# Decode attention with a running maximum, value products three steps behind the keys, and page rings of five

## Chip, core and metric

The kernel runs on one core of one Trainium2 chip. The metric is the device time of one execution in microseconds (us), the median over several executions of the same program. A core has four engines for computing that run beside each other, each with its own queue of instructions: TensorE (PE in the profile, its weight loads PEld), VectorE (DVE), ScalarE (ACT) and GpSimd (POOL). SyncE (SP) only issues transfers. Engines wait for each other through semaphores.

## What is computed

One layer of a hybrid decoder is computed for 1024 prompt tokens and for 8 sample sequences of 8 new tokens each. Only the sample attention over the paged cache is touched by the change:

```python
def diff_attend_sample(q, k, v, lam, k_past, v_past):     # 8 sequences, 8 tokens, 4 heads x 2 sub-heads
    s_past = jnp.einsum('bqhcd,bkhcd->bhcqk', q, k_past).astype(F32) * scale      # 4096 past keys
    s_new = jnp.where(jnp.tril(...), jnp.einsum('bqhcd,bkhcd->bhcqk', q, k) * scale, -jnp.inf)
    a = jax.nn.softmax(jnp.concatenate([s_past, s_new], axis=-1), axis=-1)
    w = a[:, :, 0] - lam * a[:, :, 1]
    return einsum(w[..., :P], v_past) + einsum(w[..., P:], v)
```

Each sequence has 32 pages of 128 keys and values in a pool in HBM, found through a page table. A page is 256 KB of keys and 256 KB of values. All data are 32-bit floats.

## The kernel before, in words

The program runs an input projection, the gated linear attention (to about 432 us), then `attention` (432 to 869 us), and then the dense stages (output projection, feed-forward, embedding) from 869 us to the end. Between `attention` and the dense stages stands the end of a block, which every engine has to reach.

`attention` does the prompt attention and the sample attention interleaved, in an order written out by hand: each engine has a loop over steps `t`, with `STEPS = NKV + LAG + 1`. A group is four pages of one sequence (512 keys); there are `NG = 8` groups to a sequence and `NKV = 64` groups in all. `LAG = NG + 1 = 9`, so there are 74 steps.

What belongs to the keys of group `t`, in step `t`: TensorE turns the four pages for each of four heads (`turn_keys`, line 1587, 16 transposes) into a ring of three PSUM banks; ScalarE copies heads 0 to 2 (`take_keys`, line 1470) and VectorE head 3 (line 1751) to `dec_kt`. One step later TensorE forms the scores of all heads and tokens in bank 6, `S_BANK` (`score`, line 1599). In step `t+2` VectorE takes the row maximum of that bank (line 1756) and copies it to `dec_s` (`copy_scores`, line 1762); the copy frees the bank for the next `score`. When the eight groups of a sequence and its new keys (`score_new`, `take_new`, lines 1609 and 1772) are there, VectorE forms the maximum of the whole sequence.

What belongs to the values of group `v = t - LAG`, in step `t`: ScalarE takes the exponentials from `dec_s` with that maximum as bias (`exps`, line 1481); TensorE turns them (`turn_p`, line 1622, and once per sequence `turn_new_p`, line 1616); VectorE copies them (line 1790); TensorE multiplies them with the value pages (`values`, line 1641), accumulating over all eight groups of a sequence in bank 7, `O_BANK`. At the end of a sequence VectorE scales the result (`finalize`, line 1807), TensorE merges the sub-heads (`merge`, line 1649) and ScalarE stores it (`copy_os`, line 1492).

The prompt attention has 32 units (head, block of queries), two steps for each: `prompt_scores` (line 1547), mask and maxima on VectorE (lines 1711 to 1715), `prompt_exps` (line 1446), and for the unit before `prompt_turn` (line 1560), `copy_weights` (line 1456), for the one before that `prompt_out` (line 1569). Its last piece is in step 66. The norm of its output (`norm_prompt`, line 1735) is done on VectorE in steps 68 to 71, after a logarithm and an exponential on ScalarE in step 67 (lines 1521, 1524).

The order within step `t` on TensorE: keys of heads 0 and 1, `prompt_out` (even steps) or `prompt_turn` (odd steps), keys of heads 2 and 3, `merge`, `turn_new_p`, `turn_p`, rest of `prompt_turn`, `prompt_scores`, `score`, `score_new`, `values`.

Page rings: keys and values have four slots each (`KR`, `VR`). SP loads keys (line 1302 and the next) in the order of the groups: groups 0 to 2 come before the attention starts, group 3 at its start, then the queries of two prompt units, the prompt's values `att_v` (2 MB) and the new values `dec_new_v`, and group `n` from 4 on once the keys of group `n - 4` are turned. GpSimd issues the value pages; groups 0 to 3 wait for the keys of group `2n`, later ones for the values of group `n - 4`. After the last keys SP loads two tiles of `w_out`.

The semaphore waits that matter here, quoted:

```python
1597:    pe.wait_ge(d["s_taken"], k)                              # score: S_BANK copied
1592:    pe.wait_ge(d["ring_act"], ring.emptied["keys", k, 2])    # score: keys copied
1420:    gp.wait_ge(d["ring_filled"], ring.filled(("keys", 2 * n, H - 1)))
1422:    gp.wait_ge(d["pv_done"], n - VR + 1)
```

Of the kernel before, what the change touches and what calls it, by code (L numbers as in the profile page):

```python
# [1193 lines left out]
def attention_memory(m):  # L1194
# [13 lines left out]
    m.kr, o = m.at("dec_k", o, [P, KR, 4, H * P])  # L1208
    m.vr, o = m.at("dec_v", o, [P, VR, 4, H * P])
# [4 lines left out]
    m.osc, o = m.at("dec_osc", o, [P, DV])  # L1214
# [4 lines left out]
    m.ss, o = m.at("dec_s", o, [P, PAST + NS])  # L1219
    m.kt, o = m.at("dec_kt", o, [P, 2, H, 4 * PAGE])  # L1220
    m.os, o = m.at("dec_os", o, [32, DB, DV])
# [12 lines left out]
KR, VR, QR, PRE = 4, 4, 4, 3  # L1234
NG = NPG // 4
NKV = DB * NG
LAG = NG + 1
# [18 lines left out]
class Ring:  # L1256
# [4 lines left out]
    def __init__(self):  # L1261
# [9 lines left out]
        for t in range(STEPS):  # L1271
# [11 lines left out]
            b, last = divmod(t - NG, NG)  # L1283
            if last == 0 and 0 <= b < DB:
                use(("new_s", b), "dve")
# [13 lines left out]
def load_pages(eng, ids, cache, ring, slot, sem, n):  # L1299

    for p in range(4):
        page = eng.value_load(ids[0:1, 4 * n + p:4 * n + p + 1], min_val=0, max_val=POOL - 1)
        eng.dma_start(ring[:, slot, p:p + 1, :], cache[bass.ds(page, 1)].rearrange("o t f -> t o f")).then_inc(sem, 16)  # L1303
# [15 lines left out]
def attention(nc, io, m, ps, scr, sems):  # L1319
# [12 lines left out]
    names = ("states_stored new_v_in zero_done qb_ready ring_filled ring_act ring_dve s_full s_taken mx negm exp_done "  # L1332
             "expn_done pv_done final scale_set")
# [23 lines left out]
    mx, esum, ssum, cs, negm = (m.sc[:, 24:33], m.sc[:, 34:52].rearrange("p (u g) -> p u g", u=2), m.sc[:, 52:54],  # L1357
                                m.sc[:, 54:56], m.sc[:, 56:58])
# [18 lines left out]
    with nc.Block() as block:  # L1377

        @block.sync
        def _(sp):  # L1380
# [21 lines left out]
            sp.wait_ge(s["o_done"], NU)  # L1402
# [10 lines left out]
        def _(gp):  # L1413
# [18 lines left out]
        def _(act):  # L1432
# [39 lines left out]
            def exps(v):  # L1472
                b, g = divmod(v, NG)
                if g == 0:
                    act.wait_ge(d["negm"], b + 1)
                    if b >= 2:
                        act.wait_ge(d["final"], 4 * (b - 2) + 1)
                act.wait_ge(d["s_taken"], v + 1)
                if v >= 2:
                    act.wait_ge(d["ring_filled"], ring.filled(("p", v - 2)))  # L1480
                act.activation(m.pg[:, v % 2, :], m.ss[:, 512 * g:512 * g + 512], ACT.Exp, scale=SC,
                               bias=negm[:, b % 2:b % 2 + 1], accum_out=esum[:, b % 2, g:g + 1]).then_inc(d["exp_done"], 1)
                if g == 0:
                    if b:
                        act.wait_ge(d["ring_filled"], ring.filled(("new_p", b - 1)))
                    act.activation(m.pn[:, 0:NS], m.ss[:, PAST:PAST + NS], ACT.Exp, scale=SC,
                                   bias=negm[:, b % 2:b % 2 + 1], accum_out=esum[:, b % 2, NG:NG + 1]
                                   ).then_inc(d["expn_done"], 1)
# [5 lines left out]
            for t in range(STEPS):  # L1494
                v = t - LAG
                n, c = divmod(t, 2)
                first_group = 0 <= v < NKV and v % NG == 0
                if 0 <= v < NKV and not first_group:
                    exps(v)
# [5 lines left out]
                prompt_exps(t - 1)  # L1505
                if first_group:
                    exps(v)
# [20 lines left out]
        def _(pe):  # L1528
# [49 lines left out]
            def turn_keys(t, h):  # L1578
# [7 lines left out]
                for p in range(4):  # L1586
                    ins = pe.transpose(ring_bank(key)[:, p * P:p * P + P], m.kr[:, t % KR, p, h * P:h * P + P], ident)  # L1587
                ins.then_inc(d["ring_filled"], 1)

            def score(k):  # L1590
# [5 lines left out]
                if k:  # L1596
                    pe.wait_ge(d["s_taken"], k)
# [27 lines left out]
            def values(v):  # L1625
                b, g = divmod(v, NG)
                if g == 0:
# [3 lines left out]
                    else:  # L1631
                        pe.wait_ge(d["final"], 4 * b)
                    for h in range(H):
                        pe.matmul(O_BANK[32 * h:32 * h + 32, 0:DV], m.ptn[:, 32 * h:32 * h + 32],
                                  m.vs[:, h * DV:h * DV + DV], start=True, stop=False, tile_position=(0, 32 * h),
                                  skip_group_check=True)
                pe.wait_ge(d["ring_dve"], ring.emptied["p", v])
# [1509 lines left out]
```

## Time and profile before

| what | value |
|---|---|
| three executions | 1883.73 us median (1881.60 to 1884.62) |
| span of the profiled execution | 1880.3 us |
| TensorE busy over the span | 1773.0 us (94%) |
| VectorE, ScalarE, GpSimd busy | 63%, 39%, 18% |
| attention stage (first key transpose to first instruction of the dense stages) | 433.8 to 869.3 us |
| moved by DMA between 500 and 800 us | 105.63 MB, 352 GB/s |

The end-to-end time of the profiled execution itself isn't listed; its span is 1880.3 us, and the three timed executions lie 1.3 to 4.3 us above that. In the rows, a time ahead of a group is the start in us from the span's start, "idle before" is how long the engine had nothing, with what ended that idle time. Matmuls are pipelined and overlap: the start of one to the start of the next tells more than their own durations.

### The profile page before, as it was taken

Reading aid. Unit: us, or ns where it says so; the run is one execution under the profiler, and the core shown is the slowest. Engines: PE = TensorE matmul, PEld = TensorE weight load, DVE = VectorE, ACT = ScalarE, POOL = GpSimd, SP = SyncE. Lnnn points to the kernel's source line nnn. Section 1 sums busy time; section 2 is a strip of 40 time slices with the busy share of each in tenths; the row PEclk is TensorE's granted clock in tenths of the full one; section 3 lists DMA queues with packets and bytes.
Section 4 is the critical chain, followed back from the end, with each engine's and each line's share of the span. In section 5 each row is a group of like instructions: output and inputs, shape, how many; then the busy total and the mean of one; then the engine's idle time right before and its main releaser. Section 6 shows DMA issues by size and latency. Waiting matters only on the chain.

```text
span 1880.3 us, 35481 instructions
## 1 busy us (share of the span) xinstructions
PE 1773.0 (94%) x13062; PEld 1639.1 (87%) x13062; DVE 1192.5 (63%) x1946; ACT 735.6 (39%) x1418; POOL 341.2 (18%) x360
## 2 busy tenths in 40 slices
PE   6999999996999999996999999999999999999998
PEld 6999999984666667665998999999999999999997
DVE  4223742475777777765458876667677878699443
ACT  5113322564655565653225333222323424245320
POOL 1111331001233333332111211211121000000110
PEclk9999999898999999998999999999999999999998
DMA  5323551227999999977111222222222424232121
GB/s 162 108 80 82 141 140 56 61 83 236 330 350 354 346 357 360 353 231 226 35 45 46 80 69 81 81 70 69 81 70 69 157 81 134 74 106 86 47 69 48
DMA packets 232923, 265.73 MB, mean 141 GB/s; under 512 B 16162, under 2 KB 173428, under 8 KB 232756
## 3 DMA queue, kind: packets, MB, share of 16 engines
q1 hardware_dynamic: 211988, 195.36, 33.2%
q0 software_dynamic: 20768, 68.17, 10.7%
q8 instruction: 101, 1.65, 0.4%
q14 instruction: 66, 0.54, 0.1%
HBM read 229.79 MB, written 29.21 MB: 138 GB/s over the span
## 4 chain that ended last, share of the span: by engine, by line
PE 45%; DVE 6%; ACT 1%; issue 1%; DMA 1%; POOL 0%; DVEq 0%; ACTq 0%
PE psum L2518 33%; PE psum L150 10%; DVE x_second_lo L2532 1%; DVE unit_lo L1910 1%; DMA x_first_hi_raw<-scratch_z 1%; PE psum L2197 0%; PE psum L2894 0%; DVE x_second_lo_raw L2536 0%; DVE rstd_and_products L2576 0%; DVE x_first_lo L2532 0%; DVE h L2576 0%; ACT unit_hi L1904 0%; DVE rstd_and_products L2009 0%; DVE x_lo L2226 0%; DMA w_raw<-in_w_ple_gate 0%
## 5 line engine op out<-in xcount | busy, mean ns | idle before, releaser
L2518 PE MATMUL psum<-x_second_hi,unit_hi 128*128 128x364 f32 x924 | 304.5, 330 | 8.0 <-DVE x_second_lo L2532 4.6
L2518 PE MATMUL psum<-x_second_hi,unit_lo 128*128 128x364 f32 x924 | 303.4, 328 | 0.0
L2518 PE MATMUL psum<-x_second_lo,unit_hi 128*128 128x364 f32 x924 | 303.4, 328 | 0.0
L1303 POOL DMA_DIRECT2D dec_v<-in_cache_v x256 | 137.6, 538 | 288.1 <-issue 282.2
L150 PE MATMUL psum<-x_hi,w_hi 128*128 128x364 f32 x768 | 182.0, 345 | 5.8 <-DVE x_lo L2226 5.8
L2518 PEld LDWEIGHTS psum<-x_second_hi,unit_hi 128*128 128x128 f32 x924 | 173.8, 188 | 10.8 <-issue 5.7
L2518 PE MATMUL psum<-x_first_hi,unit_hi 128*128 128x364 f32 x528 | 173.7, 329 | 0.6 <-DVE x_first_lo L2532 0.6
L2518 PEld LDWEIGHTS psum<-x_second_hi,unit_lo 128*128 128x128 f32 x924 | 174.0, 188 | 0.0
L2518 PEld LDWEIGHTS psum<-x_second_lo,unit_hi 128*128 128x128 f32 x924 | 173.7, 188 | 0.0
L2518 PE MATMUL psum<-x_first_hi,unit_lo 128*128 128x364 f32 x528 | 173.5, 329 | 0.0
L2518 PE MATMUL psum<-x_first_lo,unit_hi 128*128 128x364 f32 x528 | 173.2, 328 | 0.0
L150 PE MATMUL psum<-x_hi,w_lo 128*128 128x364 f32 x768 | 170.2, 330 | 0.0
L150 PE MATMUL psum<-x_lo,w_hi 128*128 128x364 f32 x768 | 169.8, 329 | 0.0
L1470 ACT ACTIVATE dec_kt<-psum 128x512 f32<-128x512 f32 x192 | 108.6, 599 | 154.6 <-PE psum L1587 154.6
L1904 ACT ACTIVATE unit_hi<-unit_sums 128x512 fp32r<-128x512 f32 (+1 forms) x136 | 83.3, 618 | 217.2 <-PE psum L2518 184.7
L1587 PE MATMUL psum<-consts,dec_k 128*128 128x128 f32 x1024 | 139.3, 281 | 20.2 <-DMA dec_k<-in_cache_k 8.8
L2397 POOL TENSOR_TENSOR w_raw<-w_raw,gains 128x1024 f32<-128x1024 f32 x42 | 88.7, 2111 | 379.6 <-DMA w_raw<-in_w_ffn_gate 210.8
L1904 ACT ACTIVATE unit_hi<-w_raw 128x512 fp32r<-128x512 f32 (+1 forms) x136 | 82.5, 617 | 178.2 <-PE psum L2518 155.8
L1587 PEld LDWEIGHTS psum<-consts,dec_k 128*128 128x128 f32 x1024 | 115.2, 143 | 39.2 <-issue 15.7
L150 PEld LDWEIGHTS psum<-x_hi,w_hi 128*128 128x128 f32 x768 | 131.5, 189 | 15.2 <-DVE x_lo L2226 6.2
L150 PEld LDWEIGHTS psum<-x_lo,w_hi 128*128 128x128 f32 x768 | 133.9, 189 | 0.0
L150 PEld LDWEIGHTS psum<-x_hi,w_lo 128*128 128x128 f32 x768 | 133.8, 189 | 0.0
(313 smaller groups left out, 3313.3 us busy)
## 6 DMA issues: line engine op xcount, KB each, us to landing
dec_k<-in_cache_k SPq DMA_DIRECT2D x256, 256.0 KB, 5.7
dec_v<-in_cache_v POOLq DMA_DIRECT2D x256, 256.0 KB, 5.5
w_raw<-in_w_in SPq DMA_DIRECT2D x25, 512.0 KB, 3.9
scratch_z<-ffn_hidden SPq DMA_DIRECT2D x22, 546.0 KB, 2.8
w_raw<-in_w_ffn_gate SPq DMA_DIRECT2D x22, 512.0 KB, 3.8
w_raw<-in_w_ffn_up SPq DMA_DIRECT2D x22, 512.0 KB, 3.8
w_raw<-in_w_ffn_down SPq DMA_DIRECT2D x16, 512.0 KB, 4.0
feat_swap<-feat_n SPq DMA_DIRECT2D x32, 136.5 KB, 2.4
```

The costliest lines, as they stand in the source:

```text
L150: ins = pe.matmul(out[:, c, 0:SPAN], w(k), x(k)[:, c * SPAN:c * SPAN + SPAN], start=n == 0 and w is whi and x is xhi, stop=n == len(ks) - ...
L1303: eng.dma_start(ring[:, slot, p:p + 1, :], cache[bass.ds(page, 1)].rearrange("o t f -> t o f")).then_inc(sem, 16)
L1470: act.activation(m.kt[:, t % 2, h, :], ring_bank(("keys", t, h)), ACT.Copy).then_inc(d["ring_act"], 1)
L1587: ins = pe.transpose(ring_bank(key)[:, p * P:p * P + P], m.kr[:, t % KR, p, h * P:h * P + P], ident)
L1904: act.activation(m.uhi[unit][:, 0:half_tiles(t), :], unit_source(m, t, unit), ACT.Copy).then_inc(s["w_hi"], 1)
L1910: dve.tensor_tensor(m.ulo[unit][:, 0:n, :], unit_source(m, t, unit), f32(m.uhi[unit][:, 0:n, :]), ALU.subtract).then_inc(s["w_lo"], 1)
L2397: gp.tensor_tensor(m.raw[:, u], m.raw[:, u], gain(m, "ffn").unsqueeze(2).broadcast_to([P, KT, P]), ALU.mult).then_inc(s["w_scaled"], 1)
L2518: ins = pe.matmul(bank[b], w[unit][:, j, :], x[slot][:, j, :], start=start and j == 0 and w is m.uhi and x is m.xhi7, stop=j == k - 1 and ...
L2532: dve.tensor_tensor(m.xlo7[slot][:, 0:n, :], source, f32(m.xhi7[slot][:, 0:n, :]), ALU.subtract).then_inc(s["x_lo"], 1)
```

## The change

The page rings get five slots. Slots 0 to 3 stay where they were, and slot 4 of each lies where `dec_s` (the scores of a whole sequence) was, which is gone. `LAG` is 3, `STEPS` 68. The exponentials of group `k` are taken in step `k + 2` straight from `S_BANK`, with the running maximum up to that group as bias, and their end frees the bank. The output of each group starts anew in `O_BANK`, and VectorE adds it in `dec_osc`'s neighbour `oacc`, faded by the exponential of the step in the maximum. At the end of a sequence the partial sums are weighted with `share`. The new keys of a sequence are scored at its beginning. The four `norm_prompt` stand behind the loop, and the wait ahead of the `w_out` loads is for an earlier event.

```diff
-KR, VR, QR, PRE = 4, 4, 4, 3
+KR, VR, QR, PRE = 5, 5, 4, 3
-LAG = NG + 1
+LAG = 3
...
-            sp.wait_ge(s["o_done"], NU)
+            sp.wait_ge(s["turned"], pieces_before(NU - 1))
...
             for n in range(NKV):
-                if n < VR:
-                    gp.wait_ge(d["ring_filled"], ring.filled(("keys", 2 * n, H - 1)))
-                else:
+                if 0 < n < VR:
+                    gp.wait_ge(d["ring_filled"], ring.filled(("keys", n - 1, H - 1)))
+                elif n:
                     gp.wait_ge(d["pv_done"], n - VR + 1)
...
+            def exps(k):
+                b, g = divmod(k, NG)
+                u = b % 2
+                bias = negm[:, u, g:g + 1]
+                act.wait_ge(d["negm"], k + 1)
...
+                act.activation(m.pg[:, k % 2, :], S_BANK, ACT.Exp, scale=SC, bias=bias,
+                               accum_out=esum[:, u, g:g + 1]).then_inc(d["exp_done"], 1)
                 if g == 0:
...
+                else:
+                    act.activation(fade[:, u, g:g + 1], negm[:, u, g - 1:g], ACT.Exp, scale=-1.0, bias=bias
+                                   ).then_inc(d["fade_done"], 1)
+            def shares(b):
+                act.activation(share[:, u, :], negm[:, u, :], ACT.Exp, scale=-1.0, bias=negm[:, u, NG - 1:NG]
+                               ).then_inc(d["share_done"], 1)
...
+                k = t - 2
+                prompt_exps(t - 1)
                 if t < NKV:
                     take_keys(t, 0)
                     take_keys(t, 1)
                 if c == 1 and 0 <= n - 1 < NU:
                     copy_weights(n - 1, 0)
-                prompt_exps(t - 1)
-                if first_group:
-                    exps(v)
+                if 0 <= k < NKV:
+                    exps(k)
+                    if k % NG == NG - 1:
+                        shares(k // NG)
                 if c == 0 and 0 <= n - 2 < NU:
                     copy_out(n - 2)
...
             def score(k):
-                    pe.wait_ge(d["s_taken"], k)
+                    pe.wait_ge(d["exp_done"], k)
...
             def values(v):
+                elif v:
+                    pe.wait_ge(d["summed"], v)
...
-                                        m.vr[:, v % VR, p, h * P:h * P + P], start=False, stop=g == NG - 1 and p == 3,
+                                        m.vr[v % VR][:, p, h * P:h * P + P], start=g > 0 and p == 0, stop=p == 3,
...
-                if t and t % NG == 0 and t // NG <= DB:
-                    score_new(t // NG - 1)
+                if t % NG == 1 and t // NG < DB:
+                    score_new(t // NG)
...
             def max_scores(k):
+                dve.tensor_reduce(mx, S_BANK, AX.X, ALU.max).then_inc(d["mx_done"], 1)
+                if g == 0:
+                    take_new(b)
+                dve.wait_ge(d["mx_done"], k + 1)
...
+                dve.scalar_tensor_tensor(negm[:, u, g:g + 1], mx, -SC, before, ALU.mult, ALU.min).then_inc(d["negm"], 1)
-            def copy_scores(k):
-                dve.tensor_copy(m.ss[:, 512 * g:512 * g + 512], S_BANK).then_inc(d["s_taken"], 1)
...
+            def add_output(v):
+                dve.wait_ge(d["pv_done"], v + 1)
+                if g == 0:
...
+                    dve.tensor_copy(m.oacc, O_BANK[:, 0:DV]).then_inc(d["summed"], 1)
+                else:
+                    dve.scalar_tensor_tensor(m.oacc, m.oacc, fade[:, b % 2, g:g + 1], O_BANK[:, 0:DV], ALU.mult, ALU.add
+                                             ).then_inc(d["summed"], 1)
...
                 if 0 <= t - 2 < NKV:
                     max_scores(t - 2)
-                if 0 < t - 1 <= NKV and (t - 1) % NG == 0:
-                    take_new((t - 1) // NG - 1)
-                if 0 <= t - 2 < NKV:
-                    copy_scores(t - 2)
+                if 0 < v <= NKV and v % NG:
+                    add_output(v - 1)
...
-                if HALVES < t <= HALVES + H:
-                    norm_prompt(t - HALVES - 1)
+            for h in range(H):
+                norm_prompt(h)
```

## Rows read from the trace of the kernel before

**Rows 1.** The page: its span.
```profile
span 1880.3 us, 35481 instructions
```
**Rows 2.** Stretches: start:end, length, busy by engine, granted clock, DMA share, GB/s.
```profile
464.00:800.00 336.00, 313.76 (x3796) 231.49 (x3795) 249.27 (x529) 202.62 (x520) 109.07 (x203) 1.00 1.02 348
610.00:640.00 30.00, 28.73 (x366) 21.55 (x363) 23.89 (x54) 18.54 (x49) 11.29 (x21) 1.00 1.03 372
660.00:700.00 40.00, 37.16 (x458) 27.82 (x458) 29.10 (x64) 24.78 (x65) 13.55 (x26) 1.00 1.05 356
```
**Rows 3.** Waits of TensorE's matmuls, 500 to 800 us: total, times, longest.
```profile
PE psum L1547 <- ACT att_p L1446: 7.2, 18, 0.6
PE psum L1587 <- DVE dec_s L1772: 5.8, 6, 1.0
PE psum L1616 <- ACT dec_kt L1470: 5.7, 6, 1.0
```
**Rows 4.** Transfers issued 500 to 800 us: total, KB each, us to landing.
```profile
DMA packets 47589, 105.63 MB, mean 352 GB/s; under 512 B 7048, under 2 KB 10120, under 8 KB 47532
...
dec_k<-in_cache_k SPq DMA_DIRECT2D x192, 256.0 KB, 5.7
```
**Rows 5.** Timeline at the start of the attention: start, length, instructions, idle before.
```profile
442.22 0.61 SPq L1387 DMA_DIRECT2D dec_new_v<-out_new_v_sample  x1
...
461.16 1.97 PE L1587 MATMUL psum<-consts,dec_k 128*128 128x128 f32 x8 [8.84 <-DMA dec_k<-in_cache_k]
```
**Rows 6.** Transfers issued 440 to 480 us: KB each, us to landing.
```profile
dec_new_v<-out_new_v_sample SPq DMA_DIRECT2D x1, 128.0 KB, 15.4
```
**Rows 7.** Timeline: first instruction of steps 12 and 64 on TensorE.
```profile
507.45 1.09 PE L1587 MATMUL psum<-consts,dec_k 128*128 128x128 f32 x8
...
831.28 1.16 PE L1569 MATMUL psum<-att_v,att_wt 128*128 128x128 f32 x8
```
**Rows 8.** Groups by line, 500 to 800 us: count | busy us, mean ns | idle before.
```profile
L1481 ACT ACTIVATE dec_p<-dec_s,att_small 128x512 f32<-128x512 f32 x48 | 35.2, 733 | 1.7 <-DVE att_small L1778 1.7
L1481 ACT ACTIVATION_READ_ACCUMULATOR dec_p<-dec_s,att_small 128x1 f32 x48 | 10.1, 211 | 0.0
...
L1762 DVE COPY dec_s<-psum 128x512 f32<-128x512 f32 x48 | 32.7, 681 | 0.0
L1446 ACT ACTIVATE att_p<-psum,att_small 128x512 f32<-128x512 f32 x12 | 8.4, 696 | 0.0
L1807 DVE TENSOR_SCALAR dec_osc<-psum,att_small 128x128 f32<-128x128 f32 x6 | 2.1, 350 | 0.2
```
**Rows 9.** Timeline: smallest activation; then one step (36), ScalarE and TensorE.
```profile
438.83 0.20 ACT L1514 ACTIVATE att_small<-att_small 128x2 f32<-128x2 f32 x1 [1.57 <-DVE att_small L1697]
...
659.87 0.38 ACT L1462 ACTIVATE att_o<-psum,att_small 128x128 f32<-128x128 f32 x1
...
660.13 0.49 PE L1547 MATMUL psum<-att_k,att_q 64*128 64x128 f32 x4 [0.39 <-ACT att_p L1446]
...
660.55 1.07 PE L1599 MATMUL psum<-dec_kt,dec_qb 128*32 128x512 f32 x8
```
**Rows 10.** Timeline of the end of the attention.
```profile
845.20 0.32 ACT L1521 ACTIVATE att_o_ss<-att_o_ss,eps 128x32 f32<-128x32 f32 x1
...
847.52 1.08 PE L1641 MATMUL psum<-dec_v,dec_pt 128*32 128x128 f32 x32 [0.79 <-DVE dec_pt L1790]
...
849.84 1.22 DVE L1735 TENSOR_TENSOR att_o<-att_o,att_o_ss 128x1024 f32<-128x1024 f32 x1
...
849.98 1.08 PE L1641 MATMUL psum<-dec_v,dec_pt 128*32 128x128 f32 x32 [0.79 <-DVE dec_pt L1790]
...
863.98 1.94 PE L1641 MATMUL psum<-dec_v,dec_pt 128*32 128x128 f32 x32 [2.39 <-DMA dec_v<-in_cache_v]
...
867.11 0.27 ACT L1492 ACTIVATE dec_os<-psum 32x128 f32<-32x128 f32 x1 [9.51 <-PE psum L1649]
...
869.29 1.06 ACT L2118 ACTIVATE w_hi<-w_raw 128x1024 fp32r<-128x1024 f32 x1 [1.91 <-PEq L1377]
```

More of the change, by code:

```diff
@@ L1218, in attention_memory @@
     o = O_U + 8 * TB + 32
-    m.ss, o = m.at("dec_s", o, [P, PAST + NS])
+    k4, o = m.at("dec_k_more", o, [P, KR - 4, 4, H * P])
+    v4, o = m.at("dec_v_more", o, [P, VR - 4, 4, H * P])
+    m.kr = [kr[:, r] for r in range(4)] + [k4[:, r] for r in range(KR - 4)]
+    m.vr = [vr[:, r] for r in range(4)] + [v4[:, r] for r in range(VR - 4)]
     m.kt, o = m.at("dec_kt", o, [P, 2, H, 4 * PAGE])
+    oo, o = m.at("dec_osc", o, [P, 2, DV])
+    m.oacc, m.osc = oo[:, 0], oo[:, 1]
+    m.sn, o = m.at("dec_s_new", o, [P, NS])
     m.os, o = m.at("dec_os", o, [32, DB, DV])
@@ L1282, in __init__ @@
                 use(("p", v), "dve")
-            b, last = divmod(t - NG, NG)
-            if last == 0 and 0 <= b < DB:
+            b, first = divmod(t - 1, NG)
+            if first == 0 and 0 <= b < DB:
                 use(("new_s", b), "dve")
@@ L1356, in attention @@
     neg_lam = m.sc[:, 20:21]
-    mx, esum, ssum, cs, negm = (m.sc[:, 24:33], m.sc[:, 34:52].rearrange("p (u g) -> p u g", u=2), m.sc[:, 52:54],
-                                m.sc[:, 54:56], m.sc[:, 56:58])
+    mx, mx_new, neg_new = m.sc[:, 24:25], m.sc[:, 25:26], m.sc[:, 26:27]
+    ssum, cs = m.sc[:, 52:54], m.sc[:, 54:56]
+    negm, esum, fade, share = (m.run[:, :, n, :] for n in range(4))
     def shown(i):
@@ L1470, in take_keys @@
                 act.activation(m.kt[:, t % 2, h, :], ring_bank(("keys", t, h)), ACT.Copy).then_inc(d["ring_act"], 1)
[L1472 to L1482, printed above, removed]
+            def exps(k):
[3 more added lines that the diff above has]
+                act.wait_ge(d["negm"], k + 1)
+                if k >= 2:
+                    act.wait_ge(d["ring_filled"], ring.filled(("p", k - 2)))
+                if g == 0 and b >= 2:
+                    act.wait_ge(d["final"], 4 * (b - 1))
+                act.activation(m.pg[:, k % 2, :], S_BANK, ACT.Exp, scale=SC, bias=bias,
+                               accum_out=esum[:, u, g:g + 1]).then_inc(d["exp_done"], 1)
                 if g == 0:
@@ L1586, in turn_keys @@
                 for p in range(4):
-                    ins = pe.transpose(ring_bank(key)[:, p * P:p * P + P], m.kr[:, t % KR, p, h * P:h * P + P], ident)
+                    ins = pe.transpose(ring_bank(key)[:, p * P:p * P + P], m.kr[t % KR][:, p, h * P:h * P + P], ident)
                 ins.then_inc(d["ring_filled"], 1)
@@ L1648, in merge @@
                 emptied(("merge", b))
-                pe.matmul(ring_bank(("merge", b))[0:32, 0:DV], const(m, "merge"), m.osc[:, :], start=True, stop=True
+                pe.matmul(ring_bank(("merge", b))[0:32, 0:DV], const(m, "merge"), m.osc, start=True, stop=True
                           ).then_inc(d["ring_filled"], 1)
@@ L1740, in queries @@
                 if b >= 2:
[L1741 removed]
+                    dve.wait_ge(d["s_full"], NG * (b - 1))
                 for c in range(2):
```

67 lines of the change are left out of this document (37 added, 30 removed).

## The prediction

> **What bounds it now.** I read the stretches first, to see what is at its limit in the attention stage. Between 464 and 800 us TensorE is busy 313.8 of 336 us, ScalarE 203, VectorE 249, and the DMA engines carry 348 GB/s at a share of 1.02 [rows 2]. Two resources stand close together, then, and the waits say which leads: between 500 and 800 us TensorE's matmuls wait for ScalarE's prompt exponentials, for the new scores' copy and for new exponentials (18.7 us together), never for a page [rows 3]. So TensorE, with its hand-written order, sets the pace, and the transfers follow: 105.63 MB in 300 us, each page landing 5.7 us after its issue though it is issued some four steps ahead [rows 4].
>
> The pace: step 12 begins at 507.45, step 64, the first without keys, at 831.28 [rows 7]: 323.8 us for 52 steps, 6.23 us each. In the timeline two places break it. At the start, step 4 waits 8.84 us for the pages of group 4 and begins at 461.16; SP had put the 2 MB of the prompt's values ahead of them [rows 5]. At the end, steps 64 to 73 hold nine groups of values and little else: each is a chain of exponentials, turning, copy and product, one per 2.46 us (the products that begin at 847.52 and 849.98) [rows 10], though the products are 1.08. From 831.28 to the dense stages' first instruction at 869.29 are 38.0 us [rows 7, 10].
>
> **The change, part by part.** All times are in the profiled execution, whose span is 1880.3 [rows 1]; the median of the runs is 3.4 us above that, and I add the difference to it.
>
> 1. *Fewer steps.* No matmul disappears. The values of groups 0 to 5 move out of steps 9 to 14, those of all others six steps up, so six steps' worth of values move from the bare tail to steps 3 to 8, where TensorE is the bound and pays for them. The gain isn't their work but the chains' idle time.
>
> 2. *Start.* Group 4's keys are now issued ahead of `att_v`, so step 4 would not wait for them. But step 3 now multiplies values and needs `dec_new_v`, which is still behind `att_v`. It took 15.4 us from its issue at 442.22 [rows 5, 6], to 457.6. In the new order 1 MB of keys stands ahead of both, 3.6 us of issuing more, and GpSimd's value pages come from the first moment instead of behind the keys, so the transfers share. I take 462 for its landing: 457.6 and 4 us. The ends are 452 (no wait: step 3 gets there then) and 467. Values of group 0 end at 463.4, where step 4 begins: **+2.2 us** against 461.16. The stall changes its place and keeps its size. Behind it is the fill: each step moves 8 pages and prompt keys and queries, 105.63 MB over 48 steps = 2.20 MB [rows 4]. At 356 GB/s that is 6.18 us a step against 6.08 from TensorE (below), and the rings have no lead yet. I allow **+3 us** for waits on pages over the whole stage, ends 0 and 13 (60 steps at 350 GB/s instead, 6.29 us).
>
> 3. *Sequence boundaries.* In the 52 steps six boundaries cost TensorE 5.8 us for the new scores' copy and 5.7 us for new exponentials [rows 3]. Both fall away: the new exponentials are made a step before they are turned, and `take_new` no longer follows `finalize` in the same step, so the bank is free before heads 2 and 3 ask for it. 11.5/52 = 0.22 us a step; the pace without it is 6.227 - 0.221 = 6.006 us. The work at a boundary (`score_new`, `turn_new_p`, `merge`) stays.
>
> 4. *The scores' bank.* This is the added wait. `score` waited for VectorE's copy, done early in the step; now it waits for ScalarE's exponentials, which stand behind `prompt_exps`. An exponential of 512 with its read of the sum takes 0.73 + 0.21, less some overlap: 0.84 us. Read from PSUM instead of SBUF it is no slower (0.696 against 0.733) [rows 8]. In step 36 ScalarE is through with `prompt_exps` at 659.87; the bank would be free at 660.71 + 0.06, and `score` began at 660.55 [rows 9]: 0.2 us of waiting. What hides the rest is `prompt_scores`, which TensorE starts on the same event and which takes 0.43 us at its narrowest, 1.06 at its widest. The 16 steps of the pattern of units, worked through like this one: eleven pay nothing, and five, those with wide exponentials ahead of narrow scores, pay 0.1 to 0.4 us by the durations alone, 1.21 together: 0.076 us a step. Bounds are 0 and 0.84 us in each step (cover gone). Queued behind the exponentials on ScalarE is head 2's key copy, for whose bank TensorE's next step waits: 0.94 us and the `fade` (0.20 by the smallest activation [rows 9]) later than before, but it had about 1.7 us to spare. At nothing, covered by that.
>
> 5. *VectorE.* The copy goes (0.68), the product with the step of the maximum comes (0.2) and `add_output` (0.35, like the scaling of the same 128 columns [rows 8], up to 0.45 with its wait). Even. `values` waits for the sum of the group before, done 3 us earlier in the step. Zero.
>
> Pace: 6.006 + 0.076 = **6.08 us**. Step 64 begins at 463.4 + 60 x 6.08 + 3 = 831.3, against 831.28: with values in six more steps, the same moment.
>
> 6. *Tail.* Steps 64 to 66 hold the last three groups. Step 64: piece of `prompt_out` 1.0, turning 0.6, bank and scores 1.3, values 1.1: 4.0. Step 65: the chain of 2.5 with 0.6 of prompt turning. Step 66: 2.5 and 1.1 for five blocks of `prompt_out`. Together 10.7 us to the end of the last values. In the trace of before, from there (863.98 + 1.94) to the end of `copy_os` (867.38) are 1.5 us [rows 10]; `add_output` makes it 1.9. Then the new item: `norm_prompt` lay beside the values chain and now stands alone. ScalarE's logarithm and exponential come after `copy_os`, 0.6 us, then four products of 1.22, 4.9 us with nothing beside them, and then the block's end, 1.9 us (867.38 to 869.29) [rows 10]. 10.7 + 1.9 + 0.6 + 4.9 + 1.9 and a handover of 0.1 are **20.1 us** against 38.0: -17.9. The earlier `w_out` load is worth nothing (its products by GpSimd were done before the end). GpSimd issues its last pages around 822.
>
> Sum: dense stages begin at 831.3 + 20.1 = 851.4 instead of 869.29, 17.9 earlier. 1883.7 - 17.9 = 1865.8; I say **1866**.
>
> **A rule against the change.** The trace shows 372 GB/s over 610 to 640 us with no wait for a page, and 356 over 660 to 700, when transfers are behind [rows 2]. The pace of 6.08 us asks for 2.20 MB / 6.08 = 362. The Trainium skill (HBM Reference, Specifications (TRN2)) gives about 358 GB/s for a core as its share, and about 425 for a core that streams alone. By 358 a step would be an estimated 6.15 us and the sum about 1 us later. The 372 is above that share, so it isn't a hard limit here.
>
> **Rivals.** *Transfers become the bound* (0.22): pages land late in most steps, since step and rings have no rest at boundaries any more. For: 356 GB/s when behind, share over 1. Against: 372. At 350 GB/s 60 steps last 377 us instead of 368, so 1875.
> *The start stall goes* (0.12): the new values land by 455 as pages share otherwise, steps 3 to 8 follow closely; up to 9 us less: 1857 to 1860.
> *The bank serialises ScalarE and TensorE* (0.09), the case on the other side: VectorE's running maximum comes late, or ScalarE's order leaves no cover, and `score` waits over the whole exponential. At 0.5 us a step in place of 0.08, 60 steps cost 25 us: 1891. It decides against the change from 0.08 + 17.9/60 = 0.38 us a step. Against it stand eleven of sixteen steps without a wait.
> *Nothing is gained* (0.05): late pages and the uncovered norms use up what the tail gives: 1883.
> The forecast itself, 1862 to 1870, has 0.52.
>
> **How the numbers follow.** A measurement of this kernel can tell about 0.2% from no change, 3.8 us. Faster by more: forecast, most of the transfer case and the start case: 0.85. Within: 0.05. Slower: 0.10. The range takes in the start case and the transfer case with its bound: 1856 to 1878; outside are the bank case, nothing gained, and a little at the lower end.
>
> **What would show it.** Right: TensorE waits at about 452 to 462 in the values of step 3 for `dec_new_v`, the rows for L1772 and L1616 gone from its waits, 6.1 us from step to step, `norm_prompt` back to back at the end over some 5 us. Wrong: matmuls of keys or values that wait for pages after 480 us in most steps (transfer case), or `score` with a long total of idle time behind ScalarE's exponentials (bank case).

## The result, and the profile after

The changed kernel takes 1887.6 us in the median of 20 runs (1884.0 to 1890.7), the one before 1883.2 us in 20 runs on the same chip (1878.5 to 1889.6). The ratio is 1.002, with a 95% interval of 1.0013 to 1.0028: slower by 0.2%, where 1866 (1856 to 1878) and "faster" were forecast. The profiled executions tell the same: a span of 1889.1 us against 1880.3 [rows 1].

The end of the attention first, where the gain was to be. The timeline of the kernel after, at the first instruction of step 12 on TensorE, of step 64 (L1585), then the end of the attention (columns as in [rows 5]):

```profile
525.76 0.44 PE L1603 MATMUL psum<-consts,dec_k 128*128 128x128 f32 x2
...
858.25 1.16 PE L1585 MATMUL psum<-att_v,att_wt 128*128 128x128 f32 x8
...
871.06 0.27 ACT L1508 ACTIVATE dec_os<-psum 32x128 f32<-32x128 f32 x1 [2.94 <-PE psum L1667]
...
871.83 4.63 DVE L1753 TENSOR_TENSOR att_o<-att_o,att_o_ss 128x1024 f32<-128x1024 f32 x4 [1.27 <-ACT att_o_ss L1540]
...
876.76 1.06 ACT L2158 ACTIVATE w_hi<-w_raw 128x1024 fp32r<-128x1024 f32 x1 [4.97 <-PEq L1384]
```

From step 64 to the dense stages are 18.5 us instead of 38.0: the gain is there, 19.5 us of it. But step 64 begins 27.0 us later than before, and step 12 already 18.3 us later [rows 7]. So the loss is found by comparing the times of the same steps (us; the first and the last row are moments, the others lengths):

| stretch | before | forecast | after |
|---|---|---|---|
| first key transpose | 433.81 | 433.81 | 434.94 |
| to the start of step 4 | 27.35 | 29.6 | 36.68 |
| steps 4 to 11 | 46.3 | 49.1 | 54.1 |
| steps 12 to 63 | 323.8 | 318.8 | 332.5 |
| step 64 to the dense stages | 38.0 | 20.1 | 18.5 |
| dense stages begin | 869.29 | 851.4 | 876.76 |

The three middle rows hold the miss of 25 us. In them TensorE waits as follows (waits of TensorE, 430 to 900 us: total, times, longest):

```profile
PE psum L1603 <- ACT dec_kt L1477: 17.5, 29, 2.0
PE psum L1650 <- DMA dec_new_v<-out_new_v_sample: 12.5, 1, 12.5
PE psum L150 <- DVE x_lo L2266: 9.3, 1, 9.3
PE psum L1632 <- ACT dec_os L1508: 8.5, 7, 1.3
```

And in the middle, 500 to 800 us, the stretch of [rows 3]:

```profile
PE psum L1603 <- ACT dec_kt L1477: 10.3, 20, 0.7
PE psum L1632 <- ACT dec_os L1508: 7.2, 6, 1.3
```

What is absent counts, too: no page, no score (L1615) behind ScalarE's exponentials, no copy of new scores, and prompt scores (L1563) no longer wait for prompt exponentials. In their place, transposes of keys (L1603) wait for ScalarE's copies of keys (L1477), and the turning of the new exponentials (L1632) waits still. The row of L150 is the first dense matmul's and lies behind the attention.

**The start.** The issue of the new values, then TensorE's timeline in steps 3 and 4:

```profile
447.80 4.19 SPq L1394 DMA_DIRECT2D dec_new_v<-out_new_v_sample  x1
...
455.77 1.07 PE L1615 MATMUL psum<-dec_kt,dec_qb 128*32 128x512 f32 x8
469.33 0.65 PE L1650 MATMUL psum<-dec_new_v,dec_ptn 128*32 128x128 f32 x8 [12.48 <-DMA dec_new_v<-out_new_v_sample]
469.72 1.96 PE L1659 MATMUL psum<-dec_v,dec_pt 128*32 128x128 f32 x32
471.62 1.76 PE L1603 MATMUL psum<-consts,dec_k_more 128*128 128x128 f32 x7
```

The wait is where it was forecast, but the values land at 469.3, not at 462: they are issued 5.6 us later than before (442.22 [rows 5]) and take 21.4 us instead of 15.4 [rows 6]. The transfers issued from 434 to 480 us (number, KB each, median us to landing) show why:

```profile
DMA packets 6790, 15.20 MB, mean 330 GB/s; under 512 B 861, under 2 KB 1245, under 8 KB 6785
...
dec_v<-in_cache_v POOLq DMA_DIRECT2D x22, 256.0 KB, 6.5
dec_k<-in_cache_k SPq DMA_DIRECT2D x20, 256.0 KB, 9.8
att_v<-out_new_v_prompt SPq DMA_DIRECT2D x1, 2048.0 KB, 21.3
...
dec_new_v<-out_new_v_sample SPq DMA_DIRECT2D x1, 128.0 KB, 21.4
```

The DMA engines are full (15.2 MB in 46 us), and 26 value pages are among their load (22 here and 4 of `dec_v_more`), where the kernel before had 16 and moved 14.50 MB in these 46 us. GpSimd's pages land in 6.5 us and SP's keys in 9.8 in the same stretch: two queues share the engines, and what stands last in SP's pays (21.4 us for 128 KB). The Trainium skill (DMA: Bandwidth & Descriptors, Queues, rings and completion order) says that each DMA engine takes turns between the queues it has work for; these landings agree with that.

**The pace.** One odd step (25) in the timeline, ScalarE and TensorE:

```profile
607.97 1.09 PE L1603 MATMUL psum<-consts,dec_k 128*128 128x128 f32 x8
...
609.12 0.69 ACT L1453 ACTIVATE att_p<-psum,att_small 128x512 f32<-128x512 f32 x1 [2.41 <-DVE att_small L1733]
...
609.80 1.07 ACT L1477 ACTIVATE dec_kt<-psum 128x512 f32<-128x512 f32 x2
...
610.44 0.66 PE L1603 MATMUL psum<-consts,dec_k 128*128 128x128 f32 x4 [0.51 <-ACT dec_kt L1477]
```

The keys of heads 0 and 1 are in their banks by 609.1, but ScalarE first waits for the maximum of the prompt's scores and makes their exponential. Its copy of head 0 begins at 609.80, and TensorE, whose head 3 wants head 0's bank (the ring has three), stands for 0.51 us. The diff does that with its first moved line: ahead of the key copies stood a decode exponential that was long ready, and now `prompt_exps(t - 1)` stands there, which waits for VectorE. Then a boundary step (27):

```profile
624.13 0.71 ACT L1489 ACTIVATE dec_p<-psum,dec_running 128x512 f32<-128x512 f32 x1
...
624.98 0.62 ACT L1477 ACTIVATE dec_kt<-psum 128x512 f32<-128x512 f32 x1
625.46 0.25 ACT L1508 ACTIVATE dec_os<-psum 32x128 f32<-32x128 f32 x1
625.74 0.30 PE L1632 MATMUL psum<-consts,dec_pn 128*128 128x128 f32 x1 [1.31 <-ACT dec_os L1508]
```

The ring's uses in such a step are keys 0 to 3, the merge, the new exponentials, the exponentials. Three uses ahead of the new exponentials stand the keys of head 2: their bank is what L1632 wants, and it comes free with the copy at 624.98, behind the decode's exponentials, 0.85 us of them. The trace puts the wait down to the last copy that ScalarE ended (`dec_os`).

### The profile page after: what moved, and what is told of

Its sections match the earlier page's. It is cut to its first block, busy times and chain, and to the rows that moved or that the text cites. A ratio compares the mean times of both kernels' runs of the same rounds, so it can differ in the third digit from the quotient of the medians.

```text
span 1889.1 us, 35728 instructions
## 1 busy us (share of the span) xinstructions
PE 1782.2 (94%) x13062; PEld 1640.5 (87%) x13062; DVE 1183.1 (63%) x2010; ACT 744.1 (39%) x1482; POOL 343.2 (18%) x360
## 4 chain that ended last, share of the span: by engine, by line
PE 44%; DVE 6%; ACT 1%; issue 1%; DMA 1%; POOL 0%; DVEq 0%; ACTq 0%
PE psum L2558 33%; PE psum L150 10%; DVE x_second_lo L2572 1%; DVE unit_lo L1950 1%; DMA x_first_hi_raw<-scratch_z 1%; PE psum L2237 0%; PE psum L2934 0%; DVE x_second_lo_raw L2576 0%; DVE x_first_lo L2572 0%; DVE rstd_and_products L2616 0%; DVE h L2616 0%; ACT unit_hi L1944 0%; DVE rstd_and_products L2049 0%; DVE x_lo L2266 0%; DMA w_raw<-in_w_ple_gate 0%
## 5 line engine op out<-in xcount | busy, mean ns | idle before, releaser
L150 PE MATMUL psum<-x_hi,w_hi 128*128 128x364 f32 x768 | 182.5, 346 | 9.3 <-DVE x_lo L2266 9.3
L150 PE MATMUL psum<-x_hi,w_lo 128*128 128x364 f32 x768 | 170.7, 331 | 0.0
L150 PE MATMUL psum<-x_lo,w_hi 128*128 128x364 f32 x768 | 170.3, 330 | 0.0
L1309 POOL DMA_DIRECT2D dec_v<-in_cache_v x208 | 112.2, 539 | 232.1 <-issue 229.4
L150 PEld LDWEIGHTS psum<-x_hi,w_hi 128*128 128x128 f32 x768 | 131.9, 190 | 18.6 <-DVE x_lo L2266 9.6
L1603 PE MATMUL psum<-consts,dec_k 128*128 128x128 f32 x832 | 118.5, 281 | 19.7 <-ACT dec_kt L1477 14.7
L150 PEld LDWEIGHTS psum<-x_lo,w_hi 128*128 128x128 f32 x768 | 134.3, 189 | 0.0
L150 PEld LDWEIGHTS psum<-x_hi,w_lo 128*128 128x128 f32 x768 | 134.2, 189 | 0.0
L1950 DVE TENSOR_TENSOR unit_lo<-unit_sums,unit_hi 128x512 fp32r<-128x512 f32 (+1 forms) x136 | 109.2, 809 | 27.3 <-ACT unit_hi L1944 27.3
L1603 PEld LDWEIGHTS psum<-consts,dec_k 128*128 128x128 f32 x832 | 92.5, 142 | 37.9 <-ACT dec_kt L1477 21.8
```

Source lines behind the costliest of these rows:

```text
L150: ins = pe.matmul(out[:, c, 0:SPAN], w(k), x(k)[:, c * SPAN:c * SPAN + SPAN], start=n == 0 and w is whi and x is xhi, stop=n == len(ks) - ...
L1309: eng.dma_start(ring[slot][:, p:p + 1, :], cache[bass.ds(page, 1)].rearrange("o t f -> t o f")).then_inc(sem, 16)
L1950: dve.tensor_tensor(m.ulo[unit][:, 0:n, :], unit_source(m, t, unit), f32(m.uhi[unit][:, 0:n, :]), ALU.subtract).then_inc(s["w_lo"], 1)
```

## The experiments

Each ratio is against runs of the kernel before on the same chip, whose medians were 1882.5 us for the first four kernels, 1883.9 for the next four and 1882.0 for the last three. The first four are each one edit of the kernel after, the second of them with two moves in it. The kernels are counted in the order in which they stand here (the first, the second and so on).

**Prompt exponentials back behind the key copies.**

```diff
-                prompt_exps(t - 1)
                 if t < NKV:
                     take_keys(t, 0)
...
                     copy_weights(n - 1, 0)
+                prompt_exps(t - 1)
```

> The changed kernel with prompt_exps on ScalarE back behind the copies of heads 0 and 1 and copy_weights, where it stood before the change. Theory 1 (ScalarE's new order: head 0's key copy waits behind the prompt exponentials, and head 3's transposes wait for its bank in odd steps): the pace of steps 12 to 64 falls from 6.39 to about 6.15 us, the waits of the key transposes for ScalarE's copies (17.5 us) go to under 5, and the kernel is 12 to 16 us faster than the changed one, 1872 to 1876 if the kernel before takes 1883. Rival (the scores' bank, held until the exponentials end, or the pages set the pace): score now waits for the exponentials instead, or the pages come late, and the pace stays at 6.35 to 6.45, the time within 4 us of the changed kernel.

Measured: 1879.3 us (10 runs), ratio 0.9987 (0.9977 to 0.9998). The waits of key transposes for ScalarE's key copies are gone, odd steps are back at 5.5 to 6.1 us (5.8 to 6.5 after), and the dense stages begin at 867.36. The gain, 8.3 us by the medians, is less than the 12 to 16 expected, and the pace is 6.28 us a step and not 6.15. Its waits, 500 to 800 us:

```profile
PE psum L1632 <- ACT dec_os L1508: 12.0, 6, 2.1
PE psum L1563 <- ACT att_p L1453: 4.3, 11, 0.6
PE psum L1615 <- ACT dec_p L1489: 1.0, 6, 0.2
```

Two things follow. The place of the prompt's exponentials cost some 9 us (from the first key transpose to the dense stages 432.9 us instead of 441.8). And the scores' bank, the case that I had feared, costs 1.0 us in all. But the boundary wait has grown from 1.3 to up to 2.1 us, for the prompt's exponential now stands between the copies of heads 0 and 1 and that of head 2, which comes still later.

**The start: new values first, value pages paced by the keys.** SP issues `dec_new_v` before anything else, and GpSimd's pages of group n wait for the keys of n + 1 instead of n - 1.

```diff
+            sp.dma_start(m.vs[0:NS, :], io["new_v_sample"]).then_inc(d["new_v_in"], 16)
             sp.wait_ge(ids_in, 16)
...
-                    gp.wait_ge(d["ring_filled"], ring.filled(("keys", n - 1, H - 1)))
+                    gp.wait_ge(d["ring_filled"], ring.filled(("keys", n + 1, H - 1)))
```

> The changed kernel with the new values loaded ahead of the pages at the start of the attention, and the value pages of groups 1 to 4 waiting for the keys of group n + 1 instead of n - 1. Theory (at the start the transfers are the bound and are sent in the wrong order: value pages that nobody needs yet compete with the prompt's values, and step 3 waits for a 128 KB load queued behind 2 MB): 7.8 MB have to be there for step 4, 24 us at 335 GB/s, so step 4 begins at about 461 instead of 471.6, and the kernel is 8 to 10 us faster than the changed one, 1877 to 1879. Rival (the start is bound by all bytes asked for, or what is won is given back as waits for pages in steps 5 to 12): step 4 or steps 5 to 12 wait as much, and the gain is under 3 us.

Measured: 1883.0 us (10 runs), ratio 1.000 (0.9985 to 1.0015). Step 4 begins at 457.8 instead of 471.6, 13.8 us earlier, and yet step 12 is only 4.1 us earlier: the next six steps take 6.4 to 9.4 us each. Of the 4.1, 1.6 are step 11 alone, which had a slow clock in the kernel after (last section). Against that, this kernel had the slow clock in steps 8 and 9, behind its waits for pages (0.55 from 492 to 494 us, 0.50 from 502 to 504), where it lost some 2 us. Its waits, 430 to 860 us:

```profile
PE psum L1603 <- DMA dec_k<-in_cache_k: 6.6, 4, 3.3
...
PE psum L1603 <- DMA dec_k_more<-in_cache_k: 2.4, 1, 2.4
PE psum L1585 <- DMA att_v<-out_new_v_prompt: 2.0, 1, 2.0
```

One wait for one transfer became waits for pages. Order alone gives little here: 0.2% against the changed kernel, some 4 us, where the theory had 8 to 10 and the rival less than 3.

**Rings of four.**

```diff
-KR, VR, QR, PRE = 5, 5, 4, 3
+KR, VR, QR, PRE = 4, 4, 4, 3
```

> The changed kernel with four slots in each page ring, all else as changed. Theory (the fifth slot does nothing in the steady state, where no matmul waits for a page; at the start it puts one more group of values ahead of what is needed): within 3 us of the changed kernel, 1884 to 1890, no waits for pages after step 10. Rival (the fifth slot is what keeps the pages ahead at three steps of lag): waits for pages appear in most steps, 10 us or more slower than the changed kernel.

Measured: 1883.2 us (10 runs), ratio 1.0002 (0.9989 to 1.0015). With 2 MB less to load ahead, the wait for `dec_new_v` is 6.5 us instead of 12.5. Hardly any wait for a page appears later (0.7 us in one). The fifth group in each ring brings nothing at this pace, and at the start it costs: with four, step 12 begins 86.8 us after the first key transpose instead of 90.8. Both have the slow step 11, so all 4.0 us are the start's, more than the 2.5 of the order of issue. The median, just below the 1884 to 1890 expected, fits; in the profiled execution (1887.3 us, the longest of the ten) four boundary steps with a slow clock hide it.

**Head 2's key copy ahead of the decode's exponentials.**

```diff
+                if t < NKV:
+                    take_keys(t, 2)
                 if 0 <= k < NKV:
                     exps(k)
...
-                if t < NKV:
-                    take_keys(t, 2)
```

> The changed kernel with ScalarE's copy of head 2's keys ahead of the decode exponentials instead of behind them. Theory (at the first group of a sequence turn_new_p waits 1.3 us for the bank of head 2, whose copy stands behind the exponentials): the wait ahead of turn_new_p (8.5 us in 7) falls under 2 us; the exponentials come 0.6 us later and score waits 0 to 0.3 us in some steps; the kernel is 3 to 7 us faster than the changed one. Rival (the later exponentials hold the scores' bank): score waits 0.5 us or more in most steps and the kernel is 10 us or more slower than the changed one.

Measured: 1882.8 us (10 runs), ratio 1.0006 (0.9994 to 1.0018). Waits, 430 to 860 us:

```profile
PE psum L1615 <- ACT dec_p L1489: 4.7, 20, 0.7
PE psum L1632 <- ACT dec_kt L1477: 2.5, 7, 0.5
```

The boundary wait falls from 8.5 to 2.5 us and is now named as the key copy. So the wait was for head 2's bank and not for the new exponentials. Boundary steps fall from 8.2 to 7.4 or 7.5 us, the scores' bank costs 4.7 us in their place, and the dense stages begin at 871.88. ScalarE's order trades one wait for the other.

**Both orders of banks, and on top the norms.** On the first kernel (prompt exponentials put back): the new exponentials are turned at the end of step 8b + 2 and the merge moves to the end of its step, so neither asks for a bank that was filled just before.

```diff
-                if t >= LAG + NG and (t - LAG - NG) % NG == 0:
-                    merge((t - LAG - NG) // NG)
                 if 0 <= v < NKV:
-                    if v % NG == 0:
-                        turn_new_p(v // NG)
                     turn_p(v)
...
                     values(v)
+                if t % NG == 2 and t // NG < DB:
+                    turn_new_p(t // NG)
+                if t >= LAG + NG and (t - LAG - NG) % NG == 0:
+                    merge((t - LAG - NG) // NG)
```

> The kernel of e1_prompt_exps_later with the ring of banks reordered at the boundary of two sequences: turn_new_p is issued at the end of the step before its use and merge at the end of its step, behind the values, so that neither turn_new_p nor turn_p takes the bank of head 2's keys, which ScalarE empties last. Theory (what is left of the loss at the boundaries is this wait for a bank, made longer by the exponentials that now stand ahead of head 2's copy, and the clock that falls behind it): the boundary steps go from 8.1 to 10.0 us down to 6.5 to 6.8, seven of them, and the kernel is 11 to 18 us faster than e1, 1861 to 1868 if the kernel before takes 1882. Rival (transfers: steps this short ask for more than the page loads bring): waits of keys or values for pages appear after step 12 and the gain against e1 is under 5 us.

Measured: 1872.9 us (4 runs), ratio 0.9945 (0.9929 to 0.9962), dense stages at 857.33. That is 6 to 8 us faster than the first kernel, by medians or by ratios, and not 11 to 18: the boundary steps, 8.1 to 10.0 us in the first kernel, take 7.5 and not 6.5 to 6.8. A new wait stands there, for VectorE's copy of the new exponentials, which stands near the end of its step (430 to 860 us):

```profile
PE psum L1604 <- DVE dec_ptn L1809: 11.4, 8, 1.5
```

Then heads 0 to 2 of the prompt are normed in steps 53, 55 and 57, beside TensorE, and only head 3 at the end (ScalarE's logarithm and exponential are split in the same way, in steps 52 and 67, not shown):

```diff
+                if t in (53, 55, 57):
+                    norm_prompt((t - 53) // 2)
-            for h in range(H):
-                norm_prompt(h)
+            norm_prompt(H - 1)
```

> The kernel of e5_boundary_banks with the norms of the prompt output of heads 0 to 2 done in steps 53, 55 and 57, where these heads are complete, and only head 3's behind the loop. Theory (the norms behind the loop lie bare, 1.2 us each): the dense stages begin 3.5 us earlier than in e5 and the kernel is 3 to 4 us faster. Rival (VectorE delays the running maximum in those three steps by as much): no difference to e5 beyond 1 us.

Measured: 1866.9 us (4 runs), ratio 0.9918 (0.9894 to 0.9942). Three of the four norms, bare for 4.63 us together, are under cover: from step 64 to the dense stages are 15.1 us instead of 18.7, the 3.5 that were expected. The intervals of these two kernels still overlap. On top of it, the start's order of the second experiment:

> The kernel of e6_norms_early with the order of the first loads of e2_start_order. Theory (all bytes asked for in the first twelve steps are the bound, so their order changes only where TensorE waits): step 12 begins within 3 us of where e6 has it, counted from the first key transpose, and the time is within 4 us of e6. Rival (the order matters once the steps are shorter): 5 us or more faster than e6.

Measured: 1868.5 us (4 runs), ratio 0.9919 (0.9902 to 0.9936). That is nothing: step 12 begins 87.1 us after the first transpose against 86.9, the wait for `dec_new_v` is gone, and 7.0 us for `att_v` and 7.7 us for pages of keys came in its place.

**The bytes of the start.** In the kernel after, the value pages of groups 0 to 5 are loaded with a quarter of their bytes (the first head's columns), and all heads' products of those groups read that quarter; the rest of their values is left out. The count of transfers and of matmuls stays.

```diff
+        w = P if light and n < 6 else H * P
-        eng.dma_start(ring[slot][:, p:p + 1, :], cache[bass.ds(page, 1)].rearrange("o t f -> t o f")).then_inc(sem, 16)
+        eng.dma_start(ring[slot][:, p:p + 1, 0:w], cache[bass.ds(page, 1), :, 0:w].rearrange("o t f -> t o f")).then_inc(sem, 16)
```

> The changed kernel in which the value pages of groups 0 to 5 are loaded for the first head only, a quarter of their bytes, and these groups' products use that head's values for all heads; the products are as many as before. 4.7 MB fewer move in the first ten steps. Theory (the bytes bound the start): step 12 begins 10 to 14 us earlier, counted from the first key transpose, 77 to 81 us after it instead of 90.8, and TensorE's wait in step 3 falls from 12.5 to under 6 us. Rival (the order of the queues or TensorE's own order bounds it): step 12 is less than 4 us earlier.

Measured in one run (1874.4 us), so its time alone says little; the trace is what counts. The first key transpose, the new values, and the start of step 12:

```profile
433.06 3.57 PE L1604 MATMUL psum<-consts,dec_k 128*128 128x128 f32 x16 [4.91 <-DVE att_small L1709]
...
457.78 0.66 PE L1651 MATMUL psum<-dec_new_v,dec_ptn 128*32 128x128 f32 x8 [2.94 <-DMA dec_new_v<-out_new_v_sample]
...
513.47 1.09 PE L1604 MATMUL psum<-consts,dec_k 128*128 128x128 f32 x8
```

Step 12 begins 80.4 us after the first transpose, 10.4 us sooner than after the change (90.8); 1.6 of that are the clock of step 11 again, 8.8 the bytes. Taken out are 24 pages of 192 KB, 4.7 MB, or 14 us at the 330 GB/s of this stretch, so 8.8 of their 14 us come back, though their number, their order and TensorE's work are as they were. The start waits for bytes, in the main.

**VectorE's new exponentials first.** The `take_new_p` of the early norms' kernel goes to the head of VectorE's step.

```diff
                 n, c = divmod(t, 2)
+                if 0 <= v < NKV and v % NG == 0:
+                    take_new_p(v // NG)
```

> The kernel of e6_norms_early with VectorE's copy of the turned new exponentials (take_new_p) at the very beginning of its step instead of behind finalize and the maximum. Theory (in e6 head 2's key transposes wait 1.5 us at each of eight boundaries for this copy, which empties their bank; nothing else holds them): the wait of 11.6 us falls under 1 us, the boundary steps go to 6.5 to 6.8 us, and the kernel is 8 to 12 us faster than e6, 1855 to 1860 if the kernel before takes 1883.5. Rival (the page loads become the bound at a pace of 6.1 us): waits for pages after step 12 take most of it, under 4 us faster.

Measured: 1864.7 us (4 runs), ratio 0.9899 (0.9876 to 0.9922). Boundary steps are 6.2 to 6.4 us, and the wait of 11.4 us is gone, but the span hardly moved: 1866.7 against 1865.8. Its waits, 500 to 800 us:

```profile
PE psum L1604 <- DMA dec_k<-in_cache_k: 5.8, 2, 3.7
PE psum L1564 <- ACT att_p L1454: 5.8, 16, 0.6
PE psum L1616 <- ACT dec_p L1490: 1.0, 6, 0.2
```

Now pages are late, twice: the keys of steps 26 and 41 by 2.1 and 3.7 us. Behind each of these waits TensorE's clock falls, here that of step 26 (columns as in [rows 2]):

```profile
606.00:608.00 2.00, 2.00 (x12) 2.00 (x11) 0.00 (x0) 1.90 (x6) 0.90 (x2) 0.50 1.06 367
```

Steps 26 and 41 take 8.4 and 7.4 us instead of 6.8 and 5.7. So 3.3 us of clock came on top of 5.8 us of waiting, and by the medians 2 us are left of the 8 to 12 expected. Between 464 and 800 us 358 GB/s are moved at a share of 1.04, as in the fifth kernel, where no page was late.

> The kernel of e9_new_p_first with four slots in each page ring. Theory (four slots are enough, as at the slower pace): within 3 us of e9. Rival (at 6.1 us a step, 360 GB/s, the fifth slot is what rides over slow stretches of the transfers): waits for pages in several steps and 4 us or more slower than e9.

That kernel with rings of four: 1865.4 us (4 runs), ratio 0.9904 (0.9876 to 0.9933). Pages are late six times, 7.0 us together, and the wait for `dec_new_v` is 9.4 us instead of 15.3. No difference that these runs can tell: the later waits for pages are 1.2 us more than with five slots, and step 12 begins 3.1 us sooner after the first key transpose (82.2 against 85.3).

**The banks alone.** In the kernel after, with its prompt exponentials where the change put them, the bank order and `take_new_p` as above.

> The changed kernel (prompt exponentials first on ScalarE, all norms behind the loop) with only the order of banks at the boundaries of e9_new_p_first. Theory (two separate losses: the bank of head 2's keys at the boundaries, and head 0's copy behind the prompt exponentials in odd steps): the boundary steps go from 8.2 to about 6.9 us, the odd steps stay at 6.2 to 6.5, and the kernel is 9 to 13 us faster than the changed one, about 1875. Rival (one loss, whose place only moves): within 4 us of the changed kernel.

Measured: 1875.0 us (6 runs), ratio 0.9954 (0.9936 to 0.9973). Waits, 430 to 860 us:

```profile
PE psum L1604 <- ACT dec_kt L1478: 15.0, 28, 2.2
```

Boundary steps are 6.4 to 6.6 us instead of 8.2 (or 9.8), odd steps stay at 5.8 to 6.5. The two losses of the pace are separate, one for each edit: the first kernel keeps the boundary wait and loses the wait for key copies, this one the other way round. From the first key transpose to the dense stages are 441.8 us after the change, 432.9 with the exponentials put back, 427.6 with the banks alone, 423.4 with both (the fifth kernel, which has its own wait of 11.4 us still).

## Why the prediction was wrong, step by step

The start (term 2) came out 12.1 us longer than forecast and steps 12 to 63 (terms 3 and 4) 13.7 us longer.

1. *Fewer steps*: right in kind. The steps' chains at the end were idle time and fell away.
2. *Start, +2.2 and +3 us*: the step that failed first. The place of the stall was right, its size was not: step 4 came 9.3 us later after the first transpose instead of 2.2, and steps 4 to 11 took 54.1 us instead of 49.1. I had sized the landing of `dec_new_v` at "457.6 and 4 us", by issue time and not by bytes; the issue came 5.6 us later and the landing took 6.0 us more. Six groups of values, 6.3 MB, are 18 us at 350 GB/s, and they moved from a stretch where DMA had slack (the tail: 207 GB/s at a share of 0.68 from 831 to 869 us before) to one where the keys already filled it. Step 12 came 17.2 us later than before, counted from the first transpose. The light pages show that 4.7 MB of it are worth 8.8 us, rings of four that 2 MB less asked for ahead are worth 4.0, and the second experiment that the order of issue brings only 2.5, after what its waits for pages do to the clock. Some of the 17.2 isn't bytes: step 11, the second boundary, took 9.86 us, 3.4 more than with the banks mended. The forecast had 5.1 of the 17.2; 8.8 and 3.4 make 17.3 with it, but odd steps 5, 7 and 9 are 2.0 us longer by ScalarE's order too, so these parts overlap and their sum proves nothing.
3. *Boundary waits, -0.22 us a step*: half failed. The wait for the new scores' copy went, as forecast. The wait at the turning of the new exponentials I had read by the matmul that waited, as one for new exponentials, though the row names ScalarE's key copy L1470 [rows 3]. It was a bank of the ring, freed by the copy of head 2's keys. Before, the exponentials of the first group and the new ones stood ahead of that copy; the change took them away and put those of a later group in the same place. The six boundary steps between 12 and 63 took 8.49 us in the mean, against 8.42 before. So 11.5 us of expected gain came to nothing.
4. *The scores' bank, +0.076*: right for the wait that I priced, and wrong for its neighbours. `score` waited 0 us after the change, and 1.0 us in the first experiment. The zero for head 2's copy, which "had about 1.7 us to spare", holds in plain steps and fails at boundaries. The move of `prompt_exps` ahead of the key copies stands in the diff and has no term in my sum: it costs 0.25 to 0.8 us in each odd step, 10.4 us over the 19 odd steps between 13 and 61 that aren't boundaries, by the lengths with and without it.
5. *VectorE*: even, as forecast.
6. *Tail, 20.1*: right; 18.5 measured. The norms stood bare for 4.63 us (4.9 forecast).

For steps 12 to 63 the terms nearly close: 12.0 (boundaries) and 10.4 (order), less 6.6 that I had allowed for bank and pages and that didn't come (4.0 and 2.6), are 15.8 against 13.7 us measured. Where the other 2 us are wasn't settled. Even steps are 1.5 us shorter together than in the first experiment, and the waits for prompt exponentials, 7.2 us before [rows 3] and 4.3 us in the first experiment, are gone after the change.

Of the rivals, "transfers become the bound" was right in one place that it didn't name, the start, and wrong in the steady steps: after 500 us no page was late. Only in kernels at 6.1 to 6.2 us a step do pages come late, and not in all of them (in the fifth, at 6.12, none). The rule that I weighed there, the Trainium skill's share of 358 GB/s for a core (HBM Reference, Specifications (TRN2)), met by chance exactly what the fifth and the ninth kernel moved over 336 us; the 372 of [rows 2] was a peak of 30 us and no pace to plan by. "The bank serialises ScalarE and TensorE" had the size and the sign (slower), but by luck: its mechanism was not there.

What stays open: whether a start whose value pages begin some steps later, with fewer steps between values and keys at first, would keep the short tail and spare the start. It wasn't tried. Nor is it settled why the same pauses of 0.46 and 1.31 us bring the clock down at one boundary and not at the next.

## What to carry to other kernels

When work with its own loads is moved earlier, count its bytes in the stretch where it arrives, not its instructions: a stage that is filled to the rate of its DMA pays for most of those bytes (8.8 of 14 us here), and the order of the queue won little of it back. When an engine shares a ring of banks, write down for each request whose bank it takes and where that owner's release stands in its engine's new order, at the rare steps (boundaries) too. Of a diff, each moved line needs a term of its own.

## What the hardware did that I had not expected

TensorE's clock fell inside a stage in which it was over 90% busy (311.8 of 336 us). Stretches of the kernel after around the boundary of step 11 (columns as in [rows 2]):

```profile
518.00:520.00 2.00, 0.99 (x6) 0.56 (x6) 1.36 (x3) 2.00 (x7) 1.02 (x2) 1.00 1.01 343
520.00:522.00 2.00, 1.49 (x8) 1.05 (x9) 0.98 (x2) 0.48 (x2) 0.60 (x2) 0.81 1.07 324
522.00:524.00 2.00, 2.00 (x12) 0.40 (x12) 1.07 (x2) 0.00 (x0) 0.00 (x0) 0.50 1.04 374
```

After pauses of 0.46 us (keys) and 1.31 us (L1632) the granted clock went from 1.00 to 0.50, which is 1.2 GHz, and the step's eight score matmuls took 1.93 us instead of 1.07. Such a step is 9.8 us long instead of 8.2. It isn't each boundary: two of the kernel after, four with rings of four, three in the first experiment, one in the second, none in the fourth, where the pause was at most 0.5 us, none in the fifth, where it was 1.5 us at another place, and none with the light pages, where all seven pauses of 1.3 us were as after the change. It isn't boundaries alone either: it fell behind waits for pages in the second and the ninth kernel. So where the clock falls, a short wait costs some 1.6 us more than itself. That runs of one kernel differ by it wasn't shown, for one execution of each was profiled; the mean granted clocks of the 20 runs fit (0.982 in one of 1884.1 us, 0.977 in that of 1890.7). The Trainium skill (TensorE: Matmul & The Clock Gate, A second HAM failure mode: psum-queue depth-cycling) tells of a kernel whose short idles between groups of matmuls, as it goes round its PSUM banks, make the clock oscillate; this trace agrees in kind, with pauses for a bank ahead of the fall.
